# Expert loop of a two-layer hybrid decoder: gate products into the loop's first steps, gathers eight steps ahead, row-carrying spare blocks spread out, half-wide selection tables

## The reference

```
scores = sigmoid(t @ w_r);  biased = scores + b_r
4 of 8 groups by the sum of their two best, then the 8 best of 64 experts: idx
w = scores at idx;  w = w / sum(w) * 2.5            # gates
routed = sum over e of gate[t, e] * (silu(t @ Wg[e]) * (t @ Wu[e])) @ Wd[e]
shared = (silu(t @ sg) * (t @ su)) @ sd             # all tokens
x = x + g2 * (routed + shared)
```

## Time and profile before

| | us |
|---|---|
| median of 3 runs | 1798.44 (1798.11 to 1803.48) |
| profiled execution, its time | 1797.23 |
| its span, first to last instruction | 1795.5 |

### The profile page before, as it was taken

How to read it: one execution, slowest core, us unless ns; L and a number is a source line. 1 busy time by engine, 2 the same in 40 slices (tenths; PEclk the granted TensorE clock), 3 DMA queues, 4 the chain that set the end, 5 groups by cost and what they waited for, 6 DMA issues and landing times.

```text
span 1795.5 us, 27098 instructions
## 1 busy us (share of the span) xinstructions
PE 1633.8 (91%) x10525; PEld 922.9 (51%) x10525; DVE 970.6 (54%) x2380; ACT 239.0 (13%) x607; POOL 694.1 (39%) x754
## 2 busy tenths in 40 slices
PE   6998988899999999999879989797999999999984
PEld 3774774444444444444367557644444444445443
DVE  4787466345345544444379754743444444545436
ACT  3223331000002100000031343100000000000001
POOL 1306004455445454545102240254445555455530
PEclk9898998999999999999979989898999999999996
DMA  9778466997999999999975866499999999999945
GB/s 311 224 246 286 151 262 245 416 378 269 412 409 407 390 402 394 385 375 379 325 258 188 290 208 230 162 413 415 394 393 378 390 387 401 391 377 393 395 170 215
DMA packets 216637, 588.83 MB, mean 328 GB/s; under 512 B 67705, under 2 KB 147277, under 8 KB 162622
## 3 DMA queue, kind: packets, MB, share of 16 engines
q1 hardware_dynamic: 146224, 506.99, 73.7%
q0 software_dynamic: 67232, 79.73, 13.0%
q10 hardware_dynamic: 3054, 0.38, 0.2%
HBM read 775.22 MB, written 56.95 MB: 463 GB/s over the span
## 4 chain that ended last, share of the span: by engine, by line
PE 62%; DMA 18%; DVE 10%; issue 4%; SPq 3%; POOL 1%; ACT 1%; POOLq 0%; DVEq 0%; ACTq 0%
PE ps L1390 28%; DMA xg<-hrows,idx_x 15%; PE ps L1403 12%; PE ps L1093 5%; PE ps L1239 3%; PE ps L927 3%; PE ps L983 2%; DVE xTs L2190 1%; PE ps L1351 1%; DMA ypart<-yrows_k 1%; SPq L631 1%; PE ps L991 1%; DVE ysum L2256 1%; DMA raw<-in_w_ada 1%; SPq L571 1%
## 5 line engine op out<-in xcount | busy, mean ns | idle before, releaser
L1390 PE MATMUL ps<-raw,xTs 128*64 128x256 f32 x6144 | 752.4, 397 | 22.0 <-DVE xTs L2190 15.6
L1390 PEld LDWEIGHTS ps<-raw,xTs 128*64 128x64 f32 x6144 | 419.7, 137 | 287.6 <-issue 21.2
L2190 DVE STREAM_TRANSPOSE xTs<-xg 64x256 f32<-64x256 f32 x768 | 336.7, 438 | 197.4 <-DMA xg<-hrows,idx_x 189.5
L876 POOL DMA_INDIRECT yrows_k<-ytok,idx_y x192 | 195.7, 1019 | 457.2 <-DVE ytok L2082 413.7
L1403 PE MATMUL ps<-dn,scratch 128*64 128x512 f32 x1536 | 361.5, 592 | 1.5 <-DVE scratch L2086 1.5
L869 POOL DMA_INDIRECT xg<-hrows,idx_x x192 | 202.2, 1053 | 126.5 <-DVE idx_x L2174 51.7
L2082 DVE COPY ytok<-ps 128x512 f32<-128x512 f32 x192 | 132.5, 690 | 178.9 <-PE ps L1403 178.8
L1691 ACT ACTIVATE scratch<-ps 128x128 f32<-128x128 f32 x192 | 53.2, 277 | 1117.2 <-PE ps L1390 1117.2
L1403 PEld LDWEIGHTS ps<-dn,scratch 128*64 128x64 f32 x1536 | 107.1, 135 | 146.5 <-issue 111.7
L2076 DVE TENSOR_TENSOR scratch<-scratch,ps 128x128 f32<-128x128 f32 x192 | 55.2, 288 | 234.7 <-ACT scratch L1691 233.4
L927 PEld LDWEIGHTS ps<-cst,scratch 128*128 128x128 f32 x224 | 31.1, 142 | 209.3 <-issue 123.6
(11 more groups left out here) (384 smaller groups left out, 1339.4 us busy)
## 6 DMA issues: line engine op xcount, KB each, us to landing
raw<-in_exp_w_gate SPq DMA_DIRECT2D x128, 1024.0 KB
raw<-in_exp_w_up SPq DMA_DIRECT2D x128, 1024.0 KB
dn<-in_exp_w_down SPq DMA_DIRECT2D x128, 1024.0 KB, 11.2
narrow<-in_w_ada SPq DMA_DIRECT2D x18, 1024.0 KB, 9.2
wide<-in_w_in SPq DMA_DIRECT2D x16, 1024.0 KB, 8.5
wide<-in_w_ada SPq DMA_DIRECT2D x16, 1024.0 KB, 9.4
ypart<-yrows_k SPq DMA_DIRECT2D x16, 1024.0 KB, 12.3
raw<-in_w_ada SPq DMA_DIRECT2D x14, 1024.0 KB, 12.7
```

Source lines behind the costliest of these rows:

```text
L876: pool.indirect_dma_start(yrows_k.rearrange("t (h d) -> (t h) d", h=2), bass.IndirectOffsetOnAxis(ap=idx_y[:, b:b + 1], axis=0), ytok[n % ...
L1390: ins = mm(ps[64 * h:64 * h + 64, 2 + n % 2, 0:256], xTs[n % 2][:, k, :, :].rearrange("p u i -> p (u i)"), w[:, k, h], start=k == 0, stop= ...
L2190: ins = v.transpose(xTs[n % 2][64 * e:64 * e + 64, :, u, :], xg[n % NX][64 * u:64 * u + 64, 256 * e:256 * e + 256].rearrange("p (k j) -> p ...
```

## The change

- Gate products: the part common to the three tiles becomes `gates(-1)`; it and `gates(0)` to `gates(2)` run on VectorE inside steps 1 to 4, behind `turn_x`. Their scratch moves to the place of `rowsS`, so `gates(-1)` waits for the layer's stores (`cache_stored`). The read back of the single tokens' gates moves from step 9 to step 32.
- Gathers: eight `xg` buffers, so gather n + 8 is issued in iteration n. POOL issues four gathers, then the weights of step 2 (gate and up), then four more gathers, then the down matrix of step 2, all ahead of the loop. A memset of the `rowsS` place is added at the kernel's start.
- Spare blocks: `SPARE_AT` puts spare block s at pair `bitreverse(s) + 4`. The blocks with rows stand at steps 14, 62, 38 and, in layer 1, 86; step 2 has an empty one.
- Selection tables: `pick_a` has 64 columns and three buffers. VectorE makes it with one operation a tile instead of two and no longer waits for `table_made`. TensorE multiplies each table twice, for output partitions 0 to 63 and 64 to 127, on the two column halves of the array: 16 products a tile instead of 8.

```diff
+SPARE_AT = [(int(f"{s:05b}"[::-1], 2) + 4) % SPARE for s in range(SPARE)]
+STEPS = [b for e in range(NE) for b in ([e, NE + SPARE_AT.index(e // 2)] if e % 2 == 1 else [e])]
-NRAW, NDOWN, NX, NY = 5, 4, 4, 4
+NRAW, NDOWN, NX, NY = 5, 4, 8, 4
...
+        gp.memset(placed("rowsS_all", "rowsS", 0, [P, 14 * P], F32)[:, :], 0.0)
...
-            for n in range(NX):
+            for n in range(4):
                 gather(n)
             pool.wait_ge(spare_ready.sem, spare_ready.by(layer, 1))
+            pool.wait_ge(out_first_used.sem, out_first_used.by(layer, 1))
+            for j, name in enumerate(("exp_w_gate", "exp_w_up")):
+                spare_weights(name, raw[2][:, j], 2, spare_raw)
+            for n in range(4, NX):
+                gather(n)
+            pool.wait_ge(sh_down.sem, sh_down.by(layer, KD))
+            spare_weights("exp_w_down", dn[2][:, :, :].rearrange("p j n -> p (j n)"), 2, spare_down)
...
-                if n == 9:
+                if n == 32:
                     pool.wait_ge(sgate_moved.sem, sgate_moved.by(layer, 16))
...
                 for k in range(TOPK):
-                    ins = mm(ps[:, 6, 256:256 + BLOCKS], pick_a[t % 2][0:n, k, :], pick_b[0:n, t, k, :],
-                             start=t + k == 0, stop=(t, k) == (2, TOPK - 1), skip_group_check=True)
+                    for h in range(2):
+                        ins = mm(ps[64 * h:64 * h + 64, 6, 256:256 + BLOCKS], pick_a[t][0:n, k, :], pick_b[0:n, t, k, :],
+                                 start=t + k == 0, stop=(t, k) == (2, TOPK - 1), skip_group_check=True, tile_position=(0, 64 * h))
...
-                if t == 2:
-                    W(table_made, 1)
-                for h in range(2):
-                    tt(pick_a[t % 2][0:n, :, B * h:B * h + B], iota[0:n, 0:B].unsqueeze(1).to_broadcast([n, TOPK, B]),
-                       p8[0:n, t, :].unsqueeze(2).to_broadcast([n, TOPK, B]), ALU.is_equal)
+                tt(pick_a[t][0:n, :, :], iota[0:n, 0:B].unsqueeze(1).to_broadcast([n, TOPK, B]),
+                   p8[0:n, t, :].unsqueeze(2).to_broadcast([n, TOPK, B]), ALU.is_equal)
...
-            for t in range(3):
-                gates(t)
             for n in range(2):
                 turn_x(n)
...
+                if 1 <= n <= 4:
+                    gates(n - 2)
```

More of the change, by code:

```diff
@@ L81 @@
 BLOCKS = NE + SPARE
-STEPS = [b for e in range(NE) for b in ([e, NE + e // 2] if e % 2 == 1 else [e])]
-assert NE // 2 == SPARE and sorted(STEPS) == list(range(BLOCKS))
+assert NE // 2 == SPARE == 32
+SPARE_AT = [(int(f"{s:05b}"[::-1], 2) + 4) % SPARE for s in range(SPARE)]
+STEPS = [b for e in range(NE) for b in ([e, NE + SPARE_AT.index(e // 2)] if e % 2 == 1 else [e])]
+assert sorted(STEPS) == list(range(BLOCKS))
 NSTEP = len(STEPS)
-NRAW, NDOWN, NX, NY = 5, 4, 4, 4
+NRAW, NDOWN, NX, NY = 5, 4, 8, 4
 STEP_OF_RAW = [max(range(r, NSTEP, NRAW)) for r in range(NRAW)]
@@ L91 @@
 MAIN_RAW = [[n for n in range(r, NSTEP, NRAW) if STEPS[n] < NE] for r in range(NRAW)]
+SPARE_STEPS = [n for n in range(NSTEP) if STEPS[n] >= NE]
 MAIN_DOWN = [[n for n in range(r, NSTEP, NDOWN) if STEPS[n] < NE] for r in range(NDOWN)]
@@ L341, in program @@
     ROW = PICK + 3 * TOPK * BLOCKS
-    pick_a = [scratch[:, ROW:ROW + TOPK * P].rearrange("p (k r) -> p k r", k=TOPK),
-              oT[:, :, :].rearrange("p a b -> p (a b)")[:, 0:TOPK * P].rearrange("p (k r) -> p k r", k=TOPK)]
+    pick_a = [scratch[:, ROW:ROW + TOPK * B].rearrange("p (k r) -> p k r", k=TOPK),
+              *(placed(f"pick_a{n}", "oT", TOPK * B * n, [P, TOPK, B], F32) for n in range(2))]
     order = placed("order", "bbT", 0, [P, 3, NE], F32)
@@ L355, in program @@
     dn = [placed(f"dn{n}", of, first, [P, 2, D], F32) for n, (of, first) in enumerate(down_at)]
-    xg = [placed(f"xg{n}", "cosT", 512 * n, [P, 512], F32) for n in range(NX)]
+    xg = [placed(f"xg{n}", "cosT", 512 * n, [P, 512], F32) if n < 4 else
+          placed(f"xg{n}", "scratch", PICK + 768 + 512 * (n - 4), [P, 512], F32) if n < 6 else
+          placed(f"xg{n}", "rowsS", (TOPK + 3) * NE + 512 * (n - 6), [P, 512], F32) for n in range(NX)]
     xTs = [placed(f"xTs{n}", "oT", 512 * n, [P, KD, 2, 32], F32) for n in range(2)]
@@ L878, in scatter, with spare_weights @@
                                         bounds_check=2 * T * TOPK - 1, oob_is_err=False).then_inc(y_scattered[n % NY].sem, 16)
-            def spare_weights(name, dst, o, loaded):
+            def spare_weights(name, dst, n, loaded):
+                o, place = STEPS[n] - NE, SPARE_STEPS.index(n)
                 v = "l e (p k) n -> (l e p) (k n)"
@@ L895, in _ @@
                 m = n + NRAW
[L896 to L902, removed]
                 if m < NSTEP and STEPS[m] >= NE:
@@ L905, in _ @@
                     for j, name in enumerate(("exp_w_gate", "exp_w_up")):
-                        spare_weights(name, raw[m % NRAW][:, j], STEPS[m] - NE, spare_raw)
+                        spare_weights(name, raw[m % NRAW][:, j], m, spare_raw)
                 if n == 8:
@@ L2196, in gates @@
             def gates(t):
-                if t == 0:
+                if t < 0:
+                    dve.wait_ge(cache_stored, layer + 2)
                     chain(ts(kept, order[:, :, :], 0.0, None, ALU.is_gt))
@@ L2205, in gates @@
                     chain(ins)
+                    return
                 chain(tt(gate_of, order[:, t, :].unsqueeze(1).to_broadcast([P, TOPK, NE]),
```

13 lines of the change are left out of this document (7 added, 6 removed).

## The result

| | before | after |
|---|---|---|
| median, us | 1797.82 (8 runs, 1795.98 to 1807.58) | 1787.57 (8 runs, 1784.00 to 1791.66) |
| profiled execution, us (its span) | 1797.23 (1795.5) | 1785.09 (1783.4) |

What follows compares the result with a forecast made beforehand. The prediction took late gathers, beside a parameter stall, to bound the expert loops: 37.6 us won there, 18.6 at the start and 4.0 by the clock, 60.2 off 1797.2, plus 1.2, gave 1738 us; range 1717 to 1767.

Steps and rivals of the forecast that it cites:

- every gather wait should go: Expert loops: gathers issued eight ahead end VectorE's gather waits; 37.6 of 63.5 us excess go.
- The loads of empty spare blocks: Expert loops: spare blocks without rows move no weights, so their loads were costed at nothing.
- The reserve of DMA: Expert loops: demand 396 GB/s against 412, 4% reserve; spare blocks with rows stall 10 us in layer 0, 6.5 in layer 1.
- The start: Ahead of each loop: gates out of the way, first product earlier by 9.3 us a layer, 18.6 in all.
- The clock: First steps of each loop: without the idle gap the clock doesn't fall, 2.2 + 1.8 = 4.0 us won.
- The gates in the steps: Four gate parts on VectorE inside loop steps: cost zero, or 3 us in both layers were the cover gone.
- The tables: Selection tables ahead of the loop: 1.9 us a tile on TensorE, no change; bounds -1.4 to +5.8 us a layer.
- The parameter stall: Layer 0's loop, SP busy with small parameter loads: the stall stays, 9.4 us with the slow step behind it.
- The ceiling of DMA: Rival for the loops: DMA has less than 412 GB/s, 385 being the ceiling; 1763 us, chance 0.14.
- The scatters: Rival for the loops: scatters take the gathers' place, up to 5 us late around spare blocks, 35 us; 1773, chance 0.05.
- The gathers gain nothing from depth: Rival: the gathers' queue has a fixed rate; only start, clock and POOL's small-copy stand are won; 1760, chance 0.05.
- The slower case: Rival: late spare blocks meet DMA at its slowest, at 360 GB/s the loops take 53 us more; 1829, chance 0.03.

Runs made afterwards that it cites:

- e3: Changed kernel with four gather buffers and gathers four steps ahead again, spare blocks still spread; 1788.23 us.
- e5: Changed kernel with the weight transfers of spare blocks without rows (step 2 excepted) each replaced by one of 1 KB; 1766.8 us.
- e4: Changed kernel with four gathers ahead and spare blocks in the early order of before, so only the work ahead of the loop stays changed; 1780.0 us.
- e11: The same kernel as e4, run again in a second set beside the changed kernel on one chip; 1777.27 us.
- e14: e4 with the transfers of the empty spare blocks replaced by ones of 1 KB, as in e5; 1760.18 us.
- e6: e5 with the weights of the seven spare blocks with rows also left out, so their rows' routed output is wrong; 1726.52 us.
- e1: Changed kernel with the spare blocks with rows back in front (steps 2, 5, 8, 11), all else as changed; 1785.92 us.
- e7: Changed kernel with the next layer's 33 small parameter loads issued two a step from step 24 instead of all at step 24; 1785.05 us.
- e10: e4 with the small parameter loads issued two a step (steps 24 to 40); 1774.42 us.
- e13: The changed kernel itself, run once more for comparison on one chip; 1788.33 us.
- e9: Changed kernel with six result buffers instead of four and six gather buffers instead of eight; 1789.41 us.
- e12: e6 with four gathers ahead instead of eight; 1727.86 us.

## Why the prediction was wrong

It said 1738 us and the kernel takes 1787.6. The start was right to 1.4 us a layer, the loops were wrong by 50. None of the cases that it priced lies near: its list has 1773 and then no change.

**What bounds the kernel: wrong.** The sum rests on one reading, that the excess inside the loops (37.2 and 28.5 us) comes from late gathers, because VectorE's largest wait names them. With that wait at 210.1 us (e3) and at 1.2 us (after) the time is the same. The gathers were late for the same reason as TensorE's matrices: the spare blocks' transfers. And 4.4 us of layer 0's excess, at step 48, were VectorE's work for the next layer, which deeper gathers don't touch. A wait is the cause of lost time only if nothing else is late at the same place once it is gone, and this was argued and not bounded: "every gather wait should go" is true, "what is left of the excess is the parameter stall" is not.

**The loads of empty spare blocks: the term left at zero.** "Its loads move no weights" stands in the description of the kernel, and the prediction took over from it that they cost nothing. The page of before had the sign against it: 588.83 MB moved, but 775.22 MB read from memory:

```profile
HBM read 775.22 MB, written 56.95 MB: 463 GB/s over the span
```

They cost 20.8 us by medians (e5 against after), 8.6 and 10.0 us in the two loops, and they were there before the change as well. With four gathers and early places, the form of the kernel before, they cost 17 to 20 us (e4 and e11 against e14), up to a third of the 63.5 us of excess that the forecast gave to the gathers and the parameters. No form of the change could win that back.

**The reserve of DMA: mis-sized.** The demand of 396 GB/s was right (397 measured at full pace). The forecast gave each loop 12.2 us of slack, and 4 us back between two spare blocks. It came out with 16.5 us of stalls for seven of them. Without their data the loops are 20.5 us (e5 577.3, e6 556.8) and 25.2 us (570.6, 545.4) shorter, 45.7 in all (40.3 by medians). At the forecast's 7.7 us of DMA each, three are 23.1 and four are 30.8, so by this count the slack was about 2.6 and 5.6 us for a whole loop, and what is won back between them about nil. The block at step 14 of loop 0, which shows no stall of its own, is not free either: the stall at steps 24 and 25 is 13.6 us with the spare data (e5) and 6.8 without (e6).

The 12.2 came from `dn` loads that land after 8.9 us in 1400 to 1540. TensorE had been held up by 21.6 us over the first 21 steps of that loop, but in the stretch itself it ran at full pace, as in e6, and DMA moved the same 393 GB/s. The window in before, and the one in e6:

```profile
1400.00:1540.00 140.00, 139.48 (x999) 69.18 (x1000) 69.69 (x170) 6.65 (x24) 74.74 (x75) 1.00 1.01 393
```

```profile
1400.00:1540.00 140.00, 140.00 (x1006) 69.41 (x1004) 70.04 (x173) 6.65 (x24) 64.03 (x73) 1.00 1.00 393
```

Yet in e6 they land later:

```profile
DMA to landing us min/median/max: 11.5/14.3/16.8
```

21.1 - 14.3 = 6.8 us, near the 5.6. What differs is the other queue. In the same window the kernels with the empty loads have q1 early and q0 late (after: `dn` 11.2 us, gathers 20.7), and those without have it the other way (e5: 20.3 and 7.5; e6: 14.3 and 7.0). So a short landing time on q1 alone, as in the earlier trace rows, was no measure of what DMA as a whole had left. Why next to nothing is won back between two spare blocks is not shown. In e5, DMA moves 413 GB/s in 1240 to 1320 with TensorE at full pace, so the 4% of reserve that the forecast reckoned with was there; the windows below point to one reason why it isn't enough.

Spreading the blocks over the loop won nothing that any run shows (e1 against after, 1.7 us the other way). With empty loads out of the way in both, the kernel with early places is better by 6.6 us of median (e14 against e5; by the profiled executions 5.7 in loop 0 and 6.9 in loop 1, 12.6 together). The two differ in the depth of the gathers as well, though, and with early places four gathers beat eight by 6 to 9 us (e4 and e11 against e1), so that the spreading was costed with the wrong sign is likely but not shown. Two things speak for it. One is the idle DMA at a loop's start shown above. The other is what happens behind a stall on a spare block's matrix. In windows of 3 us around step 38 of loop 1 in the kernel after (its longest stall is the 4.21 us idle ahead of 1384.34):

```profile
1379.00:1382.00 3.00, 1.13 (x10) 0.41 (x6) 0.29 (x1) 0.28 (x1) 2.39 (x3) 1.00 1.01 410
1382.00:1385.00 3.00, 0.66 (x2) 0.33 (x4) 0.00 (x0) 0.00 (x0) 1.59 (x2) 0.77 0.67 255
1385.00:1388.00 3.00, 3.00 (x11) 0.86 (x9) 0.37 (x1) 0.00 (x0) 0.00 (x0) 0.66 0.35 131
1388.00:1391.00 3.00, 3.00 (x28) 1.79 (x26) 2.19 (x6) 0.00 (x0) 1.56 (x2) 1.00 0.80 300
```

```profile
1376.29 3.84 PE L1399 MATMUL ps<-raw,xTs 128*64 128x256 f32 x32
1384.34 3.25 PE L1412 MATMUL ps<-dn,scratch 128*64 128x512 f32 x8 [4.21 <-issue]
```

TensorE waits, so it frees no buffer, so SP issues nothing, and when the late matrix lands DMA has little left to do: its share falls to 0.35, 131 GB/s, exactly where it should catch up. The granted clock falls to 0.66 as well. A reserve that exists only while TensorE waits isn't used. How much of the 6.6 us is due to which of the two, or to the depth of the gathers, was not separated.

**The start: right, with other terms.** From the first table product to the first product of loop 0, before took 287.41 - 263.43 = 23.98 us, after takes 13.26:

```profile
260.03 1.54 PE L1378 MATMUL ps<-scratch 128*64 128x96 f32 x32
261.40 2.96 PE L1378 MATMUL ps<-scratch,pick_a 128*64 128x96 f32 x64
264.29 7.39 PE L1390 MATMUL ps<-scratch,narrow 128*128 128x264 f32 x32
```

That is 10.7 us, where 9.3 was forecast. In layer 1 it is 23.98 and 13.48, so 10.5. That the sums are so near is in part luck, since the terms are others: the tables 2.8 (forecast 1.5), idle time ahead of the loop 7.81 - 1.61 = 6.2 (forecast 7.8, the turn of the rows is now the last to be ready and not the shared product), and 1.7 that the forecast didn't have: the shared product takes 7.39 us instead of 9.07. In the kernel before, the 1.44 us wait for the third table is followed by a granted clock of 0.50 (1.2 GHz) in 272 to 274, in the middle of that product:

```profile
272.00:274.00 2.00, 2.00 (x6) 1.49 (x6) 1.97 (x3) 0.86 (x4) 1.11 (x1) 0.50 0.37 156
```

After the change the wait is gone and the clock is 1.00 throughout; layer 1 shows the same, before and after. The rest of the 14.1 us ahead of loop 0 (3.4) lies ahead of the tables, where next to nothing was changed: that place moves between 259.3 and 269.5 us from kernel to kernel, so this part of the gain is luck. Between the loops as much is lost again: from the last step of loop 0 to layer 1's tables it takes 267.2 us before, 270.6 after and 268.5 to 275.1 in the other changed kernels. Why isn't shown.

**The clock: right.** The first product of each loop takes 3.85 us, against 6.06 and 5.66.

**The gates in the steps: right, cost zero.** VectorE works out a part in a step between the turns and the product of silu and up, and that product comes in time:

```profile
286.38 0.26 DVE L2205 TENSOR_SCALAR kept<-order 128x192 f32<-128x192 f32 x1
...
287.87 0.78 DVE L2211 TENSOR_SCALAR scr<-scr,gsum 128x64 f32<-128x64 f32 x3
288.68 0.29 DVE L2085 TENSOR_TENSOR scratch<-scratch,ps 128x128 f32<-128x128 f32 x1
```

It follows without idle time, so VectorE is late by what was the idle time before, and TensorE's steps 1 to 5 stay at 5.75 us.

**The tables: the wrong end of the bounds.** 32 records take 1.54 us for the first tile and 64 take 2.96 for the next two, 46 ns each, so 1.5 us a tile. Forecast were 1.9, between 1.4 (the moving columns set the pace) and 3.84 (loads and issue do). The moving columns nearly do. The Trainium skill, "TensorE: Matmul & The Clock Gate", LDWEIGHTS, gives P / 1.2 ns for a load of P columns, 53 ns for 64 as an estimate; the records follow each other in 46 ns here, so either a load is shorter than that or the loads of the two column halves overlap, and no run tells which. The Trainium skill, "TensorEngine Tiling (Array Packing)", Key Properties, says that a change of tiling mode drains the array; at 264.29, where the mode changes back, the next product starts as the last table product ends, and no gap shows. The prediction read such changes in the earlier trace rows, but both products there have the same form, 128*64. The change in a step is the turn of the activation between them, 128*128, as in the line of L927 above.

**The parameter stall: larger, and worth less.** 9.4 us were forecast to stay. The kernel after idles longer there:

```profile
428.21 3.24 PE L1399 MATMUL ps<-raw,xTs 128*64 128x256 f32 x14 [11.23 <-DMA raw<-in_exp_w_up]
```

12.7 us with the step behind it. In e6, without spare data, it is 6.8; the rest is the price of the block at step 14. e7 and e10 spread the loads and won 3 us at most, but SyncE was still held by them in e7, so what the stall itself is worth stays open.

**The sum again.** Both loops of after exceed 2 x 545.4 by 75.7 us. By e5 and e6 these are 18.6 for empty loads, 45.7 for the spare blocks' data and 11.4 that stay in loop 0 of e6: 6.8 at the parameters, 4.0 at VectorE's chain of steps 48 and 49, and the rest in small pieces. The forecast kept 25.9: nothing, 16.5 and 9.4. The difference, 49.8, is nearly the whole error of the prediction. For the profiled execution it had 1797.2 - 60.2 = 1737.0, and that took 1785.1, 48.1 more; the start won 2.6 us more than forecast and the stretch behind the loops lost 0.9. The split is good to a few us: with the loops of e13 in place of those of after, the empty loads come to 15.5.

**The rivals.** The ceiling of DMA (1763) was the right place and the wrong mechanism: the rate isn't capped at 385 GB/s, which e6 (397 at full pace) refutes, but the transfers of spare blocks find too little room in it. The scatters don't take the gathers' place (e9). "The gathers gain nothing from depth" is true (e3, e12), but not for its reason, a fixed rate of the queue; and it missed, at 1760, since it counted 16 us for POOL's stand at the small copy and nothing for the new places of the spare blocks. The slower case names the right risk, spare blocks meeting a DMA without reserve, and over-priced it.

## What to carry to other kernels

The largest wait in a profile names what came last, not what it is worth; before a deeper buffer is built for it, ask what loads the queue in front of the late transfer, and whether the next thing in line is fed by the same queue. Where MB moved and MB read differ, look for transfers that bring nothing. A stream that demands 396 GB/s, where DMA moved 411 to 418 at most in windows of some 29 us, has next to no reserve to pay extra transfers from; they go where DMA is idle (here a loop's start), and the number of them was worth more here than their place. When an edit has removed a stall, look in its trace whether the cause has only moved.

## What the runs showed of the hardware

An indirect DMA whose indices are all beyond the bounds still read 1.05 MB from memory and sent 128 packets (172.9 MB over 165 transfers in e5, 179.1 MB over 171 in e14), for 0.13 us of this kernel's time each. With these transfers in their queue the gathers landed after 20.1 us, without them after 7.5.

The DMA share stands at 1.00 to 1.02 at 382, 397 and 412 GB/s, with TensorE stalled or at full pace. It doesn't show whether DMA limits; neither does a short landing time on one of two queues (8.9 us on q1 in before, 14.3 in e6, both with TensorE at full pace and 393 GB/s).

Behind a wait of only 1.44 us of TensorE the granted clock stood at 0.50 for some 2 us, in both layers, and a product that takes 7.39 us at full clock took 9.07. The length of the wait alone doesn't tell: behind waits of 1.90 and 1.53 us in loop 0 of the same kernel (360.57 and 417.58) the next steps kept their 3.84 us.

The issue of one small load by SyncE took 16.54 us in e7 and 5.54 in the kernel after, and what SyncE had to send next stood behind it.
